# One-core encoder kernel: masks fused into CB, four projection blocks as split fp32r products, filter layers 2 and 3 later

## The reference, cut to what matters

```python
h = h + concat([ssd_out, attn_out]) @ w_out_ab      # both from rmsnorm(h) @ w_in_ab
# SSD, per direction and head, on silu(conv_centred(xbc)):
#   y_i = sum_j (C_i . B_j) * exp(a_cs_i - a_cs_j) * dt_j * x_j    (j <= i; the other direction j >= i)
# filter network:
h = sin(fr[0] * (zpos @ w1 + b1))
h = sin(fr[1] * (h @ w2 + b2))
h = sin(fr[2] * (h @ w3 + b3))
h = h @ w4
# experts:
top_v, top_i = top_k(x @ router, 2)
gates = sum(one_hot(top_i) * softmax(top_v))
out = sum_e swiglu(x, wg[e], wu[e], wd[e]) * gates[:, e]
```

## Time and profile before

| | |
|---|---|
| runs | 1636.18, 1637.4, 1643.82 us; median 1637.4 |
| profiled execution | 1638.37 us, span 1636.6 us |
| granted TensorE clock, mean | 0.985 |
| busy: PE, DVE, ACT, POOL | 98%, 76%, 60%, 5% |
| HBM read | 428.33 MB, 262 GB/s |

### The profile page before, as it was taken

How to read it: one execution, slowest core, us unless ns; L and a number is a source line. 1 busy time by engine, 2 the same in 40 slices (tenths; PEclk the granted TensorE clock), 3 DMA queues, 4 the chain that set the end, 5 groups by cost and what they waited for, 6 DMA issues and landing times.

```text
span 1636.6 us, 22040 instructions
## 1 busy us (share of the span) xinstructions
PE 1600.7 (98%) x8332; PEld 1338.1 (82%) x8332; DVE 1241.1 (76%) x1178; ACT 977.2 (60%) x888; POOL 78.1 (5%) x88
## 2 busy tenths in 40 slices
PE   8998999999999999999999999999999999999996
PEld 7765699999599587888888888888888888888885
DVE  5498556654647556988898888988988988988984
ACT  4374344432446125777677777777777677677673
POOL 0160000000302400000000000000000000000000
PEclk9999999999989999999999999999999999999999
DMA  9331155566125145999999999999999999999992
GB/s 282 103 103 52 54 158 174 179 196 190 52 96 162 52 154 189 372 370 329 361 370 335 360 370 336 360 375 336 359 370 338 358 370 336 359 371 340 354 370 113
DMA packets 221270, 430.13 MB, mean 263 GB/s; under 512 B 9530, under 2 KB 76608, under 8 KB 220896
## 3 DMA queue, kind: packets, MB, share of 16 engines
q1 hardware_dynamic: 217960, 425.34, 73.4%
q10 hardware_dynamic: 3256, 4.06, 0.8%
HBM read 428.33 MB, written 1.05 MB: 262 GB/s over the span
## 4 chain that ended last, share of the span: by engine, by line
PE 90%; DVE 5%; DMA 2%; ACT 1%; issue 1%; ACTq 0%; SPq 0%; DVEq 0%
PE ps L1627 87%; PE ps L1644 2%; DVE arena L1044 1%; DMA ring<-in_ffn_w_down_dram 1%; DVE arena L1147 0%; DVE ring_lo L1246 0%; DMA raw<-in_moe_w_up_dram 0%; DVE arena L1152 0%; DVE arena L1158 0%; DVE arena L1159 0%; DMA raw<-in_moe_w_gate_dram 0%; ACT ring_hi L820 0%; DVE arena L1180 0%; DMA arena<-in_meta_tokens_dram 0%; DVE arena L1153 0%
## 5 line engine op out<-in xcount | busy, mean ns | idle before, releaser
L1410 DVE TENSOR_TENSOR w_lo<-raw,w_hi 128x2048 fp32r<-128x2048 f32 x224 | 511.9, 2291 | 78.3 <-ACT w_hi L930 77.0
L930 ACT ACTIVATE w_hi<-raw 128x2048 fp32r<-128x2048 f32 x224 | 429.5, 1920 | 178.8 <-DMA raw<-in_moe_w_gate_dram 93.7
L1627 PE MATMUL ps<-w_hi,xg_hi 128*128 128x512 f32 x904 | 358.7, 397 | 5.5 <-DVE w_lo L1591 2.1
L1627 PE MATMUL ps<-w_hi,xg_lo 128*128 128x512 f32 x904 | 354.4, 392 | 0.0
L1627 PE MATMUL ps<-w_lo,xg_hi 128*128 128x512 f32 x904 | 353.4, 391 | 0.0
L1414 DVE TENSOR_TENSOR w_lo<-raw,w_hi 128x2048 fp32r<-128x2048 f32 x110 | 251.7, 2288 | 43.9 <-ACT w_hi L934 43.9
L934 ACT ACTIVATE w_hi<-raw 128x2048 fp32r<-128x2048 f32 x110 | 211.2, 1920 | 78.5 <-DMA raw<-in_moe_w_down_dram 77.6
L1627 PEld LDWEIGHTS ps<-w_hi,xg_hi 128*128 128x128 f32 x904 | 170.7, 189 | 40.1 <-DVE w_lo L1591 2.5
L1627 PEld LDWEIGHTS ps<-w_hi,xg_lo 128*128 128x128 f32 x904 | 170.3, 188 | 36.4
L1627 PEld LDWEIGHTS ps<-w_lo,xg_hi 128*128 128x128 f32 x904 | 170.8, 189 | 34.1
L1627 PE MATMUL ps<-w_hi,eh_hi 128*128 128x512 f32 x440 | 172.8, 393 | 2.9 <-issue 2.9
(11 more groups left out here) (299 smaller groups left out, 1888.3 us busy)
## 6 DMA issues: line engine op xcount, KB each, us to landing
raw<-in_moe_w_gate_dram SPq DMA_DIRECT2D x112, 1024.0 KB, 5.2
raw<-in_moe_w_up_dram SPq DMA_DIRECT2D x112, 1024.0 KB, 5.3
raw<-in_moe_w_down_dram SPq DMA_DIRECT2D x112, 1024.0 KB, 5.0
ring<-in_w_in_ab_dram SPq DMA_DIRECT2D x12, 1024.0 KB, 6.4
ring<-in_hy_w_in_dram SPq DMA_DIRECT2D x12, 1024.0 KB, 5.1
ring<-in_ffn_w_gate_dram SPq DMA_DIRECT2D x11, 1024.0 KB, 5.3
ring<-in_ffn_w_up_dram SPq DMA_DIRECT2D x11, 1024.0 KB, 5.3
ring<-in_ffn_w_down_dram SPq DMA_DIRECT2D x8, 1408.0 KB, 7.4
```

Of the source, the lines that this page charges most:

```text
L930: nc.scalar.activation(w_hi[:, j, :], raw[:, j, :], ACT.Copy).then_inc(sem("gu_high"), 1)
L1410: V.tensor_tensor(w_lo[:, j, :], raw[:, j, :], w_hi[:, j, :].bitcast(F32), ALU.subtract).then_inc(sem("gu_split"), 1)
L1627: return nc.tensor.matmul(o, l, r, start=start, stop=stop)
```

## The change

It does six things.

1. The products of C.B with the triangles are made once per group instead of once per head: DVE evicts each `cb` tile twice, as CB = cb * UF and CBB = cb * UB. `masks` then reads CB and POOL's W1 reads CBB, and `decay_sums` loses its two products with CB. ACT no longer evicts `cb`. POOL's W1 now waits for the `cb` tiles. In the first step the masks stand behind both heads' decay sums.
2. Blocks 2 to 5 become split products. ACT copies `xn` to `xn0_hi` behind its copy of tile 0, then the parameters, then the high part of block 2; the high parts of 3, 4 and 5 stand behind its copies of tiles 2, 3 and 5. DVE makes `xn0_lo` and the low part of block 2 ahead of everything on the parameters, and the low parts of 3, 4 and 5 behind convolutions 1, 3 and 5.
3. Filter layer 1 stays behind block 3; layer 2 moves behind `cs`, layer 3 behind `xs`, the sines with them.
4. At the experts' start the gates (`gates`) are computed behind the first `xg_lo`.
5. The last block of `ho` is made in two halves with channels 4 and 5 between them; channel 7's transposes come last, and tile `xm` is opened behind `logit` and `ss4`.
6. The twelve filling matmuls ahead of the first expert go to another bank.

The counts of the split semaphores are shifted by the four blocks (`EARLY = 4`); the moved helpers are unchanged.

```diff
     add("mlp", 0)
-    add("proj", 8, 2)
+    add("proj", 8, 4)
+    add("cs", 0, 3)
     add("mlp", 1)
-    add("proj", 10, 2)
+    add("xs", 0, 3)
     add("mlp", 2)
-    add("cs", 0, 3)
-    add("xs", 0, 3)
     add("cb", 0, 6)
...
     add("ho", 6, 2)
-    add("xm", 0, 2)
     add("logit", 0)
     add("ss4", 0)
+    add("xm", 0, 2)
     add("none", 0, 2)
...
+        ring_hi0 = [overlay(f"ring_hi0{i}", at, 2048) for i, at in enumerate((5472, 7520, 20064))]
+        xn0_hi, xn0_lo = overlay("xn0_hi", 13056, KT, T), overlay("xn0_lo", 15232, KT, T)
+        CBB = area(20064, 6, T)
...
+            if n < B_WO:
+                return ring_hi0[n % 3][:, 0:256 * k]
...
+        def split_number(n):
+            return n - 1 if n < B_WO else EARLY + n - B_FF + 1
...
                     pool.wait_ge(sem("w1_used"), h - 1)
+                pool.wait_ge(used("cb"), 3 * (h // 4) + 3)
                 for tt, (t0, n) in enumerate(TOKS):
-                    g(nc.gpsimd.tensor_scalar(W1[0:n, h % 2, tt, :], UB[0:n, tt, :], dtw[0:n, 4, 16 * tt + 8 + h:16 * tt + 9 + h],
+                    g(nc.gpsimd.tensor_scalar(W1[0:n, h % 2, tt, :], CBB[0:n, 3 * (h // 4) + tt, :], dtw[0:n, 4, 16 * tt + 8 + h:16 * tt + 9 + h],
                                               None, ALU.mult), sem("w1_ready"))
...
+                    for k in range(KT):
+                        act.wait_ge(sem("xn1_ready"), k + 1)
+                        nc.scalar.activation(xn0_hi[:, k, :], xn[:, k, :], ACT.Copy).then_inc(sem("xn_high"), 1)
                     parameters()
+                    ring_high(2)
+                if j in (2, 3):
+                    ring_high(j + 1)
+                if j == 5:
+
+                    act.wait_ge(sem("tile_ready"), NUMBER[("proj", 5)] + 1)
+                    ring_high(5)
...
-            filter_sine(0)
             for j in range(4):
                 t = ready(act, "proj", 8 + j)
                 a(nc.scalar.activation(zs[:, j, :], t[:, 0:T], ACT.Silu), used("proj"))
                 if j == 1:
-                    filter_sine(1)
-            filter_sine(2)
+                    filter_sine(0)
 
             copy("cs", 0, csr[0:HEADS, 0, :], HEADS)
             t = ready(act, "cs", 1)
...
             t = ready(act, "cs", 2)
             a(nc.scalar.activation(dtw[:, 6, 0:32], t[:, 0:32], ACT.Copy))
             a(nc.scalar.activation(dtw[0:META, 6, 32:48], t[0:META, 32:48], ACT.Copy), used("cs"))
+            filter_sine(1)
             for tt, (t0, n) in enumerate(TOKS):
                 copy("xs", tt, xT[0:n, tt, :], n, slice(0, 512))
-            for k in range(6):
-                n = TOKS[k % 3][1]
-                copy("cb", k, CB[0:n, k, :], n)
-
+            filter_sine(2)
...
+            for k in range(KT):
+                dve.wait_ge(sem("xn_high"), k + 1)
+                V.tensor_tensor(xn0_lo[:, k, :], xn[:, k, :], xn0_hi[:, k, :].bitcast(F32), ALU.subtract)
+            ring_low(2)
...
+                if j in (1, 3, 5):
+                    ring_low(3 + j // 2)
...
+            for k in range(6):
+                n = TOKS[k % 3][1]
+                t = ready(dve, "cb", k)
+                v(V.tensor_tensor(CB[0:n, k, :], t[0:n, 0:T], UF[0:n, k % 3, :], ALU.mult))
+                v(V.tensor_tensor(CBB[0:n, k, :], t[0:n, 0:T], UB[0:n, k % 3, :], ALU.mult), used("cb"))
             def masks(h):
                 for tt, (t0, n) in enumerate(TOKS):
                     dve.wait_ge(sem("w1_ready"), 3 * h + tt + 1)
-                    mult_add(W[0:n, h % 2, tt, :], UF[0:n, tt, :], dtw[0:n, 4, 16 * tt + h:16 * tt + h + 1], W1[0:n, h % 2, tt, :], sem("w1_used") if tt == 2 else None)
+                    mult_add(W[0:n, h % 2, tt, :], CB[0:n, 3 * (h // 4) + tt, :], dtw[0:n, 4, 16 * tt + h:16 * tt + h + 1], W1[0:n, h % 2, tt, :], sem("w1_used") if tt == 2 else None)
 
             def decay_sums(h):
-                m, wt = M[:, h % 4], W[:, h % 2]
+                m = M[:, h % 4]
                 dve.wait_ge(used("row"), 2 * h + 2)
                 v(V.tensor_tensor(m[:, 0:2, :], m[:, 0:2, :], RB[:, h % 2, 0:2, :], ALU.add))
                 v(V.tensor_tensor(m[0:META, 2, :], m[0:META, 2, :], RB[0:META, h % 2, 2, :], ALU.add), sem("decay_sum"))
...
-                if h == 0:
-                    dve.wait_ge(used("cb"), 6)
-                g3 = 3 * (h // 4)
-                v(V.tensor_tensor(wt[:, 0:2, :], wt[:, 0:2, :], CB[:, g3:g3 + 2, :], ALU.mult))
-                v(V.tensor_tensor(wt[0:META, 2, :], wt[0:META, 2, :], CB[0:META, g3 + 2, :], ALU.mult))
...
-                    masks(h)
+                    if step:
+                        masks(h)
                     decay_sums(h)
+                for h in (2 * step, 2 * step + 1):
+                    if not step:
+                        masks(h)
                 masked(2 * step)
...
-            dve.wait_ge(sem("gate_exp"), 1)
-            v(V.tensor_tensor(ex, ex, pick, ALU.mult))
-            v(V.tensor_reduce(m1[:, 2:4], by_tok(ex), AX.X, ALU.add))
-            v(V.reciprocal(m1[:, 4:6], m1[:, 2:4]))
-            v(V.tensor_tensor(gate3[:, :, 0:NE], by_tok(ex), over_e(m1[:, 4:6]), ALU.mult))
-            select_gates(0)
+            def gates():
+                dve.wait_ge(sem("gate_exp"), 1)
+                v(V.tensor_tensor(ex, ex, pick, ALU.mult))
+                v(V.tensor_reduce(m1[:, 2:4], by_tok(ex), AX.X, ALU.add))
+                v(V.reciprocal(m1[:, 4:6], m1[:, 2:4]))
+                v(V.tensor_tensor(gate3[:, :, 0:NE], by_tok(ex), over_e(m1[:, 4:6]), ALU.mult))
+                select_gates(0)
...
                 if first:
+                    gates()
                     later_table()
...
+            def linear_split(group, j0, n):
+                pe.wait_ge(sem("ring_split"), split_number(n))
+                w_hi_, w_lo_ = split_block(n)
+                for j in range(2):
+                    o = open_tile(group, j0 + j)
+                    for k in range(KT):
+                        m = slice(P * j, P * j + P)
+                        last = product(o[:, 0:T], w_hi_[:, k, m], w_lo_[:, k, m], (xn0_hi[:, k, :], xn0_lo[:, k, :]), k == 0, k == KT - 1)
+                    close(last)
...
-                linear("proj", 2 * n, n, xn, coming=sem("xn1_ready") if n == 0 else None)
+                if n < 2:
+                    linear("proj", 2 * n, n, xn, coming=sem("xn1_ready") if n == 0 else None)
+                else:
+                    linear_split("proj", 2 * n, n)
...
-                if n >= 3:
+                if n == 3:
                     pe.wait_ge(sem("filter_in"), 64)
-                    filter_layer(n - 3)
+                    filter_layer(0)
...
+            filter_layer(1)
...
+            filter_layer(2)
...
-            for b in range(4):
+            for b in range(3):
                 linear("ho", 2 * b, B_HO + b, xn, SEQ, coming=sem("yh_ready") if b == 0 else None)
                 if b >= 1:
                     for k in (2 * b - 2, 2 * b - 1):
                         turn_channel(k)
-                if b >= 2:
-                    for k in ((0, 1, 2, 3) if b == 2 else (4, 5)):
+                if b == 2:
+                    for k in range(4):
                         score_channel(k)
                         sum_channel(k)
-            for k in (6, 7):
+            linear("ho", 6, B_HO + 3, xn, SEQ, which=(0,))
+            for k in (4, 5):
                 turn_channel(k)
                 score_channel(k)
                 sum_channel(k)
+            linear("ho", 6, B_HO + 3, xn, SEQ, which=(1,))
+            turn_channel(6)
+            for k in (6, 7):
+                score_channel(k)
+                sum_channel(k)
+            turn_channel(7)
...
-            occupy(bank[3], 12)
+            occupy(bank[1], 12)
```

More of the change, by code:

```diff
@@ L686, in _, with ring_high @@
             act.dma_start(router[:], A["moe_router"][0].rearrange("(k p) n -> p k n", p=P)).then_inc(sem("router_in"), 16)
+            def ring_high(n, i=0, k=KT):
+                act.wait_ge(slot_in[n % RING], 16 * (n // RING + 1) + 16 * i)
+                nc.scalar.activation(high_of(n, k), ring[:, n % RING, 0:256 * k], ACT.Copy).then_inc(sem("ring_high"), 1)
             def ssd_silu(j):
@@ L1077, in _, with ring_low @@
             V.memset(crd[:, 7:8], 0.0).then_inc(used("ss1"), 1)
+            def ring_low(n, i=0, k=KT):
+                dve.wait_ge(sem("ring_high"), split_number(n) + 4 * i)
+                c = slice(0, 256 * k)
+                high = high_of(n, k)
+                V.tensor_tensor(ring_lo[:, n % RING, c], ring[:, n % RING, c], high.bitcast(F32), ALU.subtract).then_inc(sem("ring_split"), 1)
+            for k in range(KT):
+                dve.wait_ge(sem("xn_high"), k + 1)
+                V.tensor_tensor(xn0_lo[:, k, :], xn[:, k, :], xn0_hi[:, k, :].bitcast(F32), ALU.subtract)
+            ring_low(2)
             dve.wait_ge(used("param"), 1)
@@ L1239, in _ @@
                 V.memset(crd[:, 8:9], 0.0).then_inc(used("nb"), 1)
```

(7 more changed lines are left out.)

13 lines of the change are left out of this document (6 added, 7 removed).

## The result

| | before | after |
|---|---|---|
| median of five runs | 1637.4 us (1635.91 to 1643.82) | 1650.55 us (1648.46 to 1651.43) |
| profiled execution, its span | 1638.37, 1636.6 us | 1648.46, 1646.4 us |
| granted TensorE clock, mean | 0.985 | 0.978 |
| first decay sum / first row maximum | 83.76 / 142.27 us | 98.14 / 150.76 us |

The ratio is 1.0068, interval [1.0049, 1.0088]: slower, where no change clear of the noise was forecast, and outside the range. The profiled executions differ by 9.8 us of span, 8.5 of which are there at the first row maximum. Of the 1.3 behind it, 0.7 are there at the experts' first product, which comes at 635.03 instead of 625.79, and 0.6 come in the experts. The medians differ by 13.15 us, 3 more than the two profiled executions (the changed kernel's is the quickest of its five runs); no trace shows these 3.

The account below looks back on a forecast made before the run. TensorE was taken to bound the kernel, nine tenths of its chain of waits. +3.0 us at the first row maximum and -0.7 at the experts gave +2.3: 1640.7 on the profiled execution, 1639.7 against the median; range 1630 to 1647.

Parts of the forecast that it names:

- the clock: TensorE in blocks 2 to 5 and the loop: a slow stretch costs 1.0 us, cancelled against one possibly inside the 55.6.
- the bounds: Around the forecast: -3 for cheaper convolutions and earlier hand-overs, +3 for slow stretches, +4 for DVE growth, PE hiding 1.7.
- my 88.8: Time in us at which PE's first row tile was to begin, behind the cs group, filter layers, xs and cb.
- The fourth rival: Slow clock in three more stretches on PE's path (block 5, cs, loop), 1.0 each: 1642.7 us; chance 0.15.
- the loop: DVE from first decay sum to first row maximum: 50.4 us instead of 58.5, including 0.9 waiting for head 1's rows.
- The 55.6: PE's work in us from first row tile to end of tile 21, without waits; possibly holding a slow stretch.
- my 145.3: Time in us of the first row maximum, set by PE, 1.7 later than DVE; 142.27 before, so +3.0.
- set the pace: Rival: POOL's W1 triples in the loop decide from 4.5 us on; at 5.5, 1647.4 us; chance 0.08.
- The filter layers: Layers 2 and 3 leave blocks 4 and 5, 1.05 us each; layer 3's argument holds DVE to 87.5, cb evictions waiting.
- The masks: Mask loop on DVE: 1.33 us less per head, 10.6 in all, against 5.7 us of cb evictions moved to DVE.
- The experts: Start of the experts: xg_lo 0.45 us earlier by the gates' move, output projection's end 0.25 shorter; together -0.7.
- a shift between 172 and 620 us: Between the softmaxes and the experts' start: no shift expected; one there was named as a sign of being wrong.

Follow-up runs that it names:

- e4: Changed kernel with the masks of before (ACT evicts cb, each head has its two products with CB); ratio 1.0101 to the kernel before.
- e2: Changed kernel with matmuls on zeros in TensorE's waits ahead of blocks 2 to 5; ratio 1.0056 to the kernel before.
- e11: Changed kernel with 26 matmuls on zeros ahead of block 5 and two behind each of the first five thin-sum groups; ratio 1.0046 to the kernel before.
- e5: Changed kernel with blocks 2 to 5 plain fp32 and filter layers 2 and 3 back behind blocks 4 and 5; ratio 0.9961 to the kernel before.
- e8: Changed kernel with only blocks 4 and 5 split, filter arguments made earlier on DVE and layers 2 and 3 moved earlier; ratio 0.9989 to the kernel before.
- e1: Changed kernel with blocks 2 to 5 as plain fp32 products again, the rest as changed; ratio 0.9983 to the kernel before.
- e10: e8 with ten matmuls on zeros, two behind each of the first five groups of thin sums; ratio 0.9970 to the kernel before.
- e3: Changed kernel with only blocks 4 and 5 split, 2 and 3 plain fp32; ratio 0.9995 to the kernel before.
- e7: e6 with the wide sums ahead of block 5 and the thin ones between its second tile's products; ratio 0.9988 to the kernel before.
- e6: e3 with filter layer 2 behind block 5 and layer 3 behind the cumulative sums; ratio 1.0004 to the kernel before.
- e9: e5 with the end of the output projection and the filling bank as in the kernel before; ratio 0.9963 to the kernel before.

## Why the prediction was wrong, step by step

**The step that failed** is the clock, as I put it: one slow stretch "inside it is likely", "I let the two cancel and keep 1.0 for the bounds". In the profiled execution two stretches on PE's path ahead of the row tile cost much more than 1.0 each:

- Block 5: 2.4 us, 8.7 against 6.3 us for 48 records. This one is shown: the changed kernel and e4 leave the wait of 6.3 us empty and have 8.7 and 9.0; e2 and e11 fill it and have 6.3.
- From the sums to the row tile: 18.3 us where I had 15.6. In e5 and before it is 13.4 with no filter layer in it; two layers at full clock (0.7 each) and the wait of 0.59 make 15.4. The other 2.9 I put down to the clock of 0.54 (the 13.4 of before already hold a stretch of 3.4 us). But e4, with the same products, takes 15.54 from the sums to the row tile, as I had it: these 2.9 belong to the profiled execution, and how often the kernel pays them no profile here says.

Together 5.3, and the row tile's 94.15 is 5.35 above my 88.8; the small rest cancels (a block at full clock 0.4 dearer, block 5 started 0.1 sooner, 0.2 too much of mine behind the sums). My price of 1.0 was that of a 16 us group of fp32 blocks, of which the slow stretch covers only the first 2.6 us; in block 5 it covers 5.4 us and costs more than twice that. The mean clock of each run says that the profile is no exception: 0.976 to 0.978 in all five runs of the changed kernel, 0.980 to 0.985 in e2, 0.978 to 0.987 in e11, and 0.978 to 0.989 in the runs of before that were timed with the experiments. The fourth rival had the mechanism with the same wrong price: its three stretches gave 1642.7, and with the 5.3 in place of its 3.0 it would have been 1645.0. Its third stretch, in the loop, did not come: the clock is 1.00 there.

The Trainium skill ("TensorE: Matmul & The Clock Gate", The HAM clock gate) has an idle array fall to 1.2 GHz. Block 5 behind its wait of 6.3 us bears that out, in the changed kernel and in e4, and I held it against the change, but gave it "1.0 more". Block 3 goes both ways: behind a wait of 1.82 us it ran at 1.00 in the changed kernel, behind 2.70 at 0.77 in e4, and e11, behind 2.52, had 0.76 there. And what the rule says of idleness does not cover the thin sums: in e8 PE is busy for 5.00 of 5.00 us at a clock of 0.50.

**A second term was too small**: the loop, which I put at 50.4 us for DVE, took 52.6. The wait for head 1's rows is 1.74 instead of 0.9. The products of the masks have a mean of 570 ns instead of 534, 0.9 us for the 24 of them, and the small decay sums 589 instead of 540. The large masked products grew as well, 924 instead of 726, but the small ones gave nearly all of it back (529 instead of 718). POOL is busy for 58% of this loop and for 46% of the old one; that it is the cause was not tested. I had this growth in the bounds, with the remark that PE hides 1.7 of it. PE hid nothing, because its own work was shorter than I had it: 53.1 us from the row tile to the end of tile 21, without its wait, instead of 55.6. The 55.6 held what I suspected there, a stretch at 1.2 GHz, in which eight records took 3.71 us that take 2.10 in the changed kernel (before):

```profile
121.35 3.71 PE L1627 MATMUL ps<-arena,ktab 128*128 128x272 f32 x8
```

```profile
121.00:125.00 4.00, 4.00 (x13) 2.82 (x10) 3.75 (x8) 3.27 (x7) 0.00 (x0) 0.57 0.30 105
```

So DVE was last at the maximum, and PE waited 1.24 us for it at 149.20. The errors add up to the 5.5 us between 150.76 and my 145.3: 5.35 at the row tile, less 0.4 of my margin between the row tile and the decay sum, plus 2.2 in the loop, less the 1.7 by which I had PE behind DVE. Two of my errors hide one another here: with PE's work at 55.6, PE alone would have been at the maximum near 150.7, without any growth on DVE.

**What held:** the landing and the low part (36.6 against 36.3); the first convolution 37.92 (37.7), the last to end at 72.2 (72.4); block 5's start 67.17 (67.3). The waits ahead of blocks 2, 3 and 4 are 2.1, 1.8 and 0.5 instead of 3.0, 4.5 and 0.8: PE came to block 2 at 34.6 instead of 33.3, and block 2 itself took 8.7 us instead of 5.9, so its slow stretch was hidden. A split block at full clock takes 6.3, not 5.9. POOL does not set the pace. The filter layers: I had the cb evictions wait for the third argument, but never priced the move on its own; e1 against e5 puts it at 2.75 us.

**The masks** are worth 5.3 us at the maximum when nothing else is changed in the first 180 us (e5); the 5.5 of e4, on top of the splits, has clock stretches of its own in it. I had 8.1 for the shorter loop and 1.5 back for the evictions, 6.6.

**The experts:** the gates' move gives 0.31 instead of 0.45. The reordered end of the output projection, forecast at -0.25, costs 0.28: of that, 0.17 is a gap ahead of channel 7's scores (in the changed kernel from 622.20 to 622.81 where such a step takes 0.45). DVE makes that channel's slice from 622.40 to 622.75, and the transposes that used to stand there now come behind; the rest is spread. In all -0.03 instead of -0.7.

**After the maximum** the change lost 1.3 us more, 8.5 to 9.8, where I had it gain 0.7. I took a shift between 172 and 620 us as none; 0.8 come between the maximum and the first router scores. From 180 to 200 us the clock is 0.74 in the changed kernel and 1.00 before. e5, e8, e10 and others have such stretches between 150 and 190 us too, each elsewhere. Why the kernel before has none there in its profile is open; it may be part of why e5's profile shows only 2.0 us less span than that of before, though its median is 5.9 us lower than that of the runs of before that were timed with it.

**What stays open:** why the thin sums leave TensorE at 1.2 GHz for as long as they do. By the clock record of the traces the stretches around them last 10.2 to 13.7 us in the changed kernel, e2, e3, e7 and e8, 6.8 in e6 and e10, 6.8 and another 3.4 in e1, and 3.4 in before, e4, e5, e9 and e11 (there 5 us behind them). Before, e5 and e9 have plain fp32 blocks and the filter layers among them; e4 has neither, and the TensorE program of the changed kernel, so the order of the products alone does not set the length. Each kernel has one profile here, and none says how much the length varies from one execution to the next. What is common: in every profile but e11's, the one with block 5's wait and the sums filled, a stretch begins during the thin products or within 0.2 us of their end.

## What to carry to other kernels

Before work is shortened on an engine, ask when its operands come: a split that saves 1.3 us of TensorE a block costs more than that once the block waits for the making of its parts, and what waited for 6.3 us then began at half speed. Price a slow stretch by what lies in it at that level (here 2.4 us for a block), look for thin products, and take more than one profile before a stretch is put down to an edit. And mind what is moved onto the path ahead of an eviction: the move of two small filter layers took half of what the masks gained.

## What was not expected of the hardware

- TensorE fell to 1.2 GHz without a wait: in e8 it is busy for all of 70 to 80 us at a granted clock of 0.50 and 0.51, from early in the 36 records with 8 columns on. They take 4.13 us at full clock in e5 and 6.05 there. In all thirteen profiles a stretch also begins between 32.5 and 36.1 us, during the 48 records with 16 columns or within 1 us of their end.
- Two executions of the same products differed: e4 had 3.4 us at 1.2 GHz behind the sums and a slow part in block 3, the changed kernel 10.2 us and none. Ten matmuls on zeros between the thin products, 2.1 us of added work, cost e11 nothing at the row tile against e2 (91.94 and 92.11).
- A POOL triple became quicker with the change (3.66 and 3.83 us, 4.11 before), while DVE's 128x544 masked products became slower (924 ns, 726 before).
